# Where TensorE's combination and gather stand in an expert step, and which engine makes two low parts

## The reference, cut to what matters

```python
for e in range(N_EXPERTS):                      # 32 experts, D = 1024, FF = 512
    gate, up = jnp.split(z @ w_gate_up[e], 2, axis=-1)
    y = y + combine[..., e:e + 1] * ((jax.nn.silu(gate) * up) @ w_down[e])
return rms_norm(x + y, final_norm_g)
```

## Time and profile before

| | |
|---|---|
| median of 3 runs | 925.91 us |
| the profiled execution's own time | 929.3 us |
| its span | 927.5 us |
| TensorE matmul busy | 873.3 us (94%) |
| VectorE busy | 814.4 us (88%) |
| ScalarE busy | 621.7 us (67%) |
| 96 loads of expert weights, 2 MB each, median from issue to landing | 9.8 us |

### The profile page before, as it was taken

One profiled execution on the slowest core, in us unless ns is written; L12 is line 12 of the kernel. 1 busy time (PEld: TensorE's weight loads), 2 busy tenths in 40 slices (PEclk: granted clock), 3 DMA queues, 4 the chain that ended last, 5 costly groups with the idle time before them and its releaser, 6 DMA issues.

```text
span 927.5 us, 14508 instructions
## 1 busy us (share of the span) xinstructions
PE 873.3 (94%) x5734; PEld 751.2 (81%) x5734; DVE 814.4 (88%) x818; ACT 621.7 (67%) x537; POOL 11.0 (1%) x19
## 2 busy tenths in 40 slices
PE   5999999999999899868999999999999999999975
PEld 5999999999899899657877777777777877777764
DVE  5358999999867957488999999999999999999993
ACT  5563434345453573558888878888888878887882
POOL 0110000000000000020000000000000000000000
PEclk9999999999999999979999999999999999999997
DMA  9952545455443486518999999999999999999911
GB/s 379 374 183 97 210 155 194 170 184 194 159 155 119 182 317 267 211 37 327 384 400 399 411 395 407 398 411 400 401 408 408 396 400 406 409 398 396 423 66 45
DMA packets 20146, 270.64 MB, mean 292 GB/s; under 512 B 2192, under 2 KB 2448, under 8 KB 3856
## 3 DMA queue, kind: packets, MB, share of 16 engines
q1 hardware_dynamic: 19696, 268.59, 73.0%
q10 hardware_dynamic: 416, 1.57, 0.5%
HBM read 269.10 MB, written 1.05 MB: 291 GB/s over the span
## 4 chain that ended last, share of the span: by engine, by line
PE 48%; DVE 30%; issue 14%; ACT 6%; DMA 1%; DVEq 1%; SPq 0%; ACTq 0%
DVE lo L932 10%; PE ps L1317 10%; PE ps L1146 9%; PE ps L1147 9%; PE ps L1148 9%; DVE lo_last L932 7%; ACT hi L578 5%; PE ps L1305 3%; DVE lo L704 2%; DVE conv L791 2%; PE ps L1161 2%; PE ps L1163 2%; PE ps L1162 2%; DVE y_lo L1055 1%; DVE hT L1041 1%
## 5 line engine op out<-in xcount | busy, mean ns | idle before, releaser
L932 DVE TENSOR_TENSOR lo<-raw,hi 128x2048 fp32r<-128x2048 f32 x142 | 323.5, 2287 | 7.6 <-ACT hi L578 6.6
L578 ACT ACTIVATE hi<-raw 128x2048 fp32r<-128x2048 f32 x141 | 264.2, 1909 | 3.5 <-PE ps L1317 3.5
L1317 PE MATMUL ps<-hi,xeT 128*128 128x512 f32 x384 | 158.4, 412 | 15.1 <-DVE lo L932 11.2
L704 DVE TENSOR_TENSOR lo<-raw,hi 128x2048 fp32r<-128x2048 f32 x62 | 141.7, 2288 | 30.0 <-ACT hi L396 28.5
L1146 PE MATMUL ps<-inA,hi 128*128 128x256 f32 x576 | 165.1, 287 | 1.6 <-DVE lo L704 1.1
L1147 PE MATMUL ps<-inA,hi 128*128 128x256 f32 x576 | 163.8, 284 | 0.0
L1148 PE MATMUL ps<-inA,lo 128*128 128x256 f32 x576 | 163.7, 284 | 0.0
L396 ACT ACTIVATE hi<-raw 128x2048 fp32r<-128x2048 f32 x63 | 120.6, 1914 | 63.6 <-PE ps L1148 41.0
L1317 PE MATMUL ps<-lo,xeT 128*128 128x512 f32 x384 | 150.7, 392 | 0.0
L1146 PEld LDWEIGHTS ps<-inA,hi 128*128 128x128 f32 x576 | 111.4, 193 | 2.7 <-DVE lo L704 2.6
L1147 PEld LDWEIGHTS ps<-inA,hi 128*128 128x128 f32 x576 | 111.5, 194 | 0.1
(11 more groups left out here) (214 smaller groups left out, 1229.5 us busy)
## 6 DMA issues: line engine op xcount, KB each, us to landing
raw<-in_w_experts SPq DMA_DIRECT2D x96, 2048.0 KB, 9.8
raw<-in_w_dense SPq DMA_DIRECT2D x29, 2048.0 KB, 7.8
raw<-in_w_dense SPq DMA_DIRECT2D x2, 1024.0 KB, 8.1
x_sb<-in_x SPq DMA_DIRECT2D x1, 1024.0 KB, 4.8
mem_sb<-in_mem SPq DMA_DIRECT2D x1, 1024.0 KB, 15.5
x_again<-in_x ACTq DMA_DIRECT2D x1, 1024.0 KB, 5.0
out<-x SPq DMA_DIRECT2D x2, 512.0 KB, 2.7
ffn_row<-in_rows ACTq DMA_DIRECT2D x1, 512.0 KB, 7.4
```

The lines of the kernel that those rows point to most:

```text
L578: nc.scalar.activation(expert_half(hi, N0), raw_flat(slot, k % 2), ACT.Copy).then_inc(hi_made, 1)
L704: nc.vector.tensor_tensor(conv_half(lo, N), raw_half(slot, h), conv_half(hi, N).bitcast(f32), ALU.subtract).then_inc(lo_made, 1)
L932: nc.vector.tensor_tensor(expert_half(lo, N0), raw_flat(expert_slot(m), k % 2), expert_half(hi, N0).bitcast(f32), ALU.subtract).then_inc(l ...
L1317: last = mm(dst, xeT[:, par, 4 * (k % 2) + kt, k // 2 % 2, :], expert_half(w, N)[:, kt * 512:(kt + 1) * 512], start=(k % 4 == 0 and kt == ...
```

## The change

Two low parts leave VectorE. For the rows, TensorE multiplies the high part with minus the identity and adds this onto the gathered sum, which is still in its bank (`xeT_remainder`, between halves 6 and 7, two matmuls of 512 columns); the bank then holds the low part, and ScalarE copies it out (`expert_xeT_lo`). The same is done for the output (`y_remainder`, between halves 2 and 3, two matmuls; `y_out_lo` on ScalarE, two copies). ScalarE makes the minus identity once, before step 0. The combination is cut in two, after half 3 and after half 4; the gather is cut in 3 + 5 of its 8 tiles, before and after half 5. `hT_hi` and `hT_lo` move from the end of a step to behind high (low) 4 of the next, and `y_hi` behind high 2. After the loop three of the four down halves come before step 14's combination. For this the gather sets `start` only for the first tile of each bank, since the later minus identity matmuls add to all of it.

TensorE after: halves 0, 1, 2, output's remainder, 3, combination (first half), 4, combination (second half), gather 0 to 2, 5, gather 3 to 7, weights and `put`, 6, rows' remainder, 7, and on as before. ScalarE after: high 2, `y_hi`, 3, 4, `hT_hi`, 5, 6, two `y_lo`, gate out, 7, 8, rows' high part, `put`, 9, rows' low part, 10, up out, 11, SiLU, 12, 13. VectorE after: low 2, 3, 4, `hT_lo`, 5 to 8, slot weights, 9, `pick`, 10, 11, 12, `h`, 13.

The diff, cut to its core:

```diff
@@ -603,16 +606,28 @@
             nc.scalar.activation(ident_bf[:, :], ident, ACT.Copy).then_inc(ident_made, 1)
+            nc.scalar.activation(minus_ident[:, :], ident, ACT.Copy, scale=-1.0).then_inc(ident_made, 1)
             expert_xeT(0, 0)
-            def y_out(i, used):
+            def expert_xeT_lo(i, par):
+                act.wait_ge(xeT_rest, i)
+                nc.scalar.activation(xeT[:, par, :, :, SLOTS:2 * SLOTS], gathered_view(), ACT.Copy).then_inc(xeT_made, 1)
+            def y_out_lo(count):
+                act.wait_ge(y_rest, count)
+                for g in range(2):
+                    nc.scalar.activation(y_lo[g][:, :], DN[g], ACT.Copy).then_inc(y_lo_made, 1)
+            def y_out(used):
...
-            def hT_hi(i):
-                act.wait_ge(h_made, i + 1)
+            def hT_hi(count):
+                act.wait_ge(h_made, count)
                 nc.scalar.activation(hT[:, :, :, 0:SLOTS], h_sb[:, :, :, :], ACT.Copy).then_inc(h_hi, 1)
@@ -628,24 +643,35 @@
                 if start:
-                    more(4, 5)
+                    more(4, 5, 6)
                 else:
-                    more(2, 3, 4, 5)
+                    more(2)
+                    if not isinstance(j, int):
+                        y_out(used)
+                    more(3, 4)
+                    act.wait_ge(half_used, used)
+                    hT_hi(i)
+                    more(5, 6)
+                    if not isinstance(j, int):
+                        y_out_lo(i - 1)
                 act.wait_ge(half_used, used + 4)
...
                 nc.scalar.activation(gu_sb[:, 0:FF], G0, ACT.Copy).then_inc(gate_out, 1)
-                more(6, 7)
                 if start:
+                    more(7)
                     act.wait_ge(comb_made, 1)
                     act.wait_ge(loops_made, 1)
+                else:
+                    more(7, 8)
                 expert_xeT(i + 1, (r + 1) % 2)
-                more(8)
...
                 nc.scalar.activation(put[:, r, :], G0[:, T:2 * T], ACT.Copy).then_inc(put_made, 1)
+                if start:
+                    more(8)
                 more(9)
+                expert_xeT_lo(i + 1, (r + 1) % 2)
                 if not start:
@@ -660,10 +686,6 @@
                     more(12, 13)
-                    act.wait_ge(half_used, used + 12)
-                hT_hi(i)
-                if not start:
-                    y_out(i - 1, used + 12)
@@ -672,7 +694,11 @@
                 step(j, 1)
+            act.wait_ge(half_used, 2 * STEP * last_turn + (DENSE + 2 * STEP - 4))
+            hT_hi(2 * last_turn + 2)
+            y_out(2 * STEP * last_turn + (DENSE + 2 * STEP - 4))
             expert_hi(last_turn, 2 * STEP - 4, 2)
+            y_out_lo(2 * last_turn + 1)
             expert_hi(last_turn, 2 * STEP - 4, 3)
@@ -1034,10 +1060,10 @@
-            def hT_lo(i):
-                dve.wait_ge(h_made, i + 1)
-                dve.wait_ge(h_hi, i + 1)
+            def hT_lo(count):
+                dve.wait_ge(h_made, count)
+                dve.wait_ge(h_hi, count)
                 nc.vector.tensor_tensor(hT[:, :, :, SLOTS:2 * SLOTS], h_sb[:, :, :, :], hT[:, :, :, 0:SLOTS].bitcast(f32),
@@ -1068,10 +1094,14 @@
                 else:
-                    more(2, 3, 4, 5, 6, 7)
-                xeT_lo(i + 1, (r + 1) % 2)
+                    more(2)
+                    more(3, 4)
+                    hT_lo(i)
+                    more(5, 6, 7, 8)
                 slot_weights(i, r)
-                more(8, 9)
+                if start:
+                    more(8)
+                more(9)
                 make_pick(r, slice(r + 2, r + 3) if first else bass.ds(2 * j + (r + 2), 1))
@@ -1083,11 +1113,6 @@
                     more(13)
-                hT_lo(i)
-                if not start:
-                    dve.wait_ge(y_hi_made, i)
-                    for g in range(2):
-                        y_out_lo(g, DN[g], y_lo_made)
@@ -1096,6 +1121,7 @@
                 step(j, 1)
+            hT_lo(2 * last_turn + 2)
             expert_lo(last_turn, 2 * STEP - 4, 2)
@@ -1293,10 +1319,10 @@
-            def gather(i, par):
+            def gather(i, par, tiles=range(KT)):
                 pe.wait_ge(pick_made, i + 1)
-                for c in range(KT):
+                for c in tiles:
                     dst = ps[:, 6 + c // 4, c % 4 * 2 * SLOTS:(c % 4 + 1) * 2 * SLOTS]
@@ -1304,8 +1330,9 @@
                                   pick2[:, par, t, 0:2 * SLOTS],
-                                  start=(k == 0), stop=(k == 3 * TT - 1))
-                last.then_inc(gathered, 1)
+                                  start=(k == 0 and c % 4 == 0), stop=(k == 3 * TT - 1), skip_group_check=True)
+                if c == KT - 1:
+                    last.then_inc(gathered, 1)
@@ -1333,14 +1360,31 @@
-            def combine(par):
-                for t in range(TT):
+            def combine(par, tiles=range(TT)):
+                for t in tiles:
                     for g in range(2):
...
+            def y_remainder(count):
+                pe.wait_ge(y_hi_made, count)
+                for g in range(2):
+                    last = mm(DN[g], minus_ident[:, :], y_hi[:, g * 512:(g + 1) * 512], start=False, stop=True,
+                              skip_group_check=True)
+                last.then_inc(y_rest, 1)
+            def xeT_remainder(i, par):
+                pe.wait_ge(xeT_hi, i + 1)
+                for a in range(2):
+                    last = mm(DN[a], minus_ident[:, :],
+                              xeT[:, par, 4 * a:4 * a + 4, :, 0:SLOTS].rearrange("p c x s -> p (c x) s"),
+                              start=False, stop=True, skip_group_check=True)
+                last.then_inc(xeT_rest, 1)
@@ -1356,19 +1400,24 @@
                 gate_or_up(j, at_half, 1, r)
+                gate_or_up(j, at_half, 2, r)
+                if not first:
+                    y_remainder(i - 1)
+                gate_or_up(j, at_half, 3, r)
                 if not first:
...
                     pe.wait_ge(y_lo_made, 2 * i - 2)
-                    combine(r)
-                gate_or_up(j, at_half, 2, r)
-                gate_or_up(j, at_half, 3, r)
-                gather(i + 1, (r + 1) % 2)
+                    combine(r, (0,))
                 if not start:
...
                 gate_or_up(j, at_half, 4, r)
+                if not first:
+                    combine(r, (1,))
+                gather(i + 1, (r + 1) % 2, (0, 1, 2))
                 gate_or_up(j, at_half, 5, r)
+                gather(i + 1, (r + 1) % 2, (3, 4, 5, 6, 7))
@@ -1388,6 +1437,9 @@
                 gate_or_up(j, at_half, 6, r)
+                if start:
+                    pe.wait_ge(ident_made, 2)
+                xeT_remainder(i + 1, (r + 1) % 2)
                 gate_or_up(j, at_half, 7, r)
@@ -1418,14 +1470,17 @@
+            y_remainder(2 * last_turn + 1)
+            pe.wait_ge(silu_made, 2 * last_turn + 2)
+            pe.wait_ge(h_made, 2 * last_turn + 2)
+            pe.wait_ge(h_lo, 2 * last_turn + 2)
+            down(last_turn, 2 * STEP - 4, 0, 0, (G0, G1))
+            down(last_turn, 2 * STEP - 4, 1, 0, (G0, G1))
+            down(last_turn, 2 * STEP - 4, 2, 1, (G0, G1))
             pe.wait_ge(put_made, 2 * last_turn + 1)
...
             combine(0)
-            pe.wait_ge(silu_made, 2 * last_turn + 2)
-            pe.wait_ge(h_made, 2 * last_turn + 2)
-            pe.wait_ge(h_lo, 2 * last_turn + 2)
-            for k in range(4):
-                down(last_turn, 2 * STEP - 4, k, k // 2, (G0, G1))
+            down(last_turn, 2 * STEP - 4, 3, 1, (G0, G1))
             pe.wait_ge(put_made, 2 * last_turn + 2)
...
             combine(1)
```

More of the change, by code:

```diff
@@ L147, in hybrid_moe_kernel @@
         fold2 = at("fold2", S0 + 2 * KB + 512, [2, SLOTS])
+        minus_ident = at("minus_ident", S0 + 4 * KB, [P], r32)
         part = at("part", S0, [2, T])
@@ L210, in hybrid_moe_kernel @@
         silu_made, h_made, h_hi, h_lo = map(sem, ("silu_made", "h_made", "h_hi", "h_lo"))
+        xeT_rest, y_rest = sem("xeT_rest"), sem("y_rest")
         y_hi_made, y_lo_made, combined = map(sem, ("y_hi_made", "y_lo_made", "combined"))
```

## The result

The changed kernel takes **941.0 us** (median of 4 runs, 940.36 to 941.75) against 926.38 us for the kernel before, measured again beside it (4 runs, 925.41 to 927.47). The ratio is 1.0158, with a 95% interval of 1.014 to 1.0175: slower by 1.6%, inside the predicted range and 1.3 us above the predicted 939.7. Its profiled execution took 940.36 us with a span of 938.6 us.

A forecast was written before the change was run, and what follows sets the result against it. VectorE was taken to bound the kernel at 31.20 us a step. 929.3 + 17.9 (loop) + 0.5 (first steps) - 4.6 (end) = 943.1 us, or 939.7 against the median; range 932 to 947.

The forecast's parts named there:

- What bounded the kernel before: In the loop, VectorE sets the pace at 31.20 us a step and TensorE follows; about 2.3 comes off VectorE.
- The new wait and its cycle: In each loop step, TensorE waits about 2 us for y_lo; the cycle through ScalarE and the gather takes 32.48 us.
- The second cycle: TensorE's own cycle in the loop: half 11, y_hi, y_lo, rest of the step, 32.2 us; the longer one was taken.
- In the loop: Steps 2 to 15: each 1.28 us longer than 31.20, times 14, +17.9 us.
- Steps 0 and 1: Before the loop: later gather and rows plus two remainder matmuls cost +0.5 us, bounds -1 and +3.
- The end to the last combination: After the loop: halves now precede the combination, 14.6 us instead of 19.1, -4.6; -1.9 if the clock drops.
- the 3.4 by which I corrected its time to the median: Whole kernel: the profiled execution is 3.4 us above the runs' median 925.91, so 943.1 becomes 939.7.
- Nothing of VectorE's is late next: In the loop after the change, lows 9 to 12 come 2 us or more ahead of TensorE.
- The faster case: In the loop, y_lo copies are ready when half 3 ends, TensorE sets the pace: 912 us; chance 0.08.
- The falling clock: Clock falls in every loop step after the gap, 2.7 us a step, 38 more, 977 us; chance 0.04.

The follow-up runs named there:

- run 9: Kernel before with only the rows' low part moved (minus identity on TensorE between halves 6 and 7, copy on ScalarE behind high 9, gather's start flags): 913.88 us.
- run 1: Changed kernel with ScalarE's two y_lo copies moved from behind high 6 to ahead of high 5: 933.22 us.
- run 2: Changed kernel with ScalarE's two y_lo copies moved between high 5 and high 6: 923.84 us.
- run 3: Changed kernel with ScalarE's two y_lo copies moved later, behind the gate's copy and high 7: 1005.52 us.
- run 4: Changed kernel with TensorE running all of the combination after half 4, ScalarE untouched: 923.99 us.
- run 6: Changed kernel with ScalarE's high 9 moved ahead of the rows' high part, y_lo still behind high 6: 935.89 us.
- run 7: Changed kernel with both the y_lo copies between high 5 and high 6 and high 9 ahead of the rows' high part: 909.73 us.
- run 10: Run 7 with VectorE's product h moved behind low 13: 912.75 us.
- run 8: Changed kernel with the combination of step 14's output ahead of the last four down halves again, loop untouched: 943.38 us.

## Why the prediction was right

**What bounded the kernel before** was read rightly: run 9 takes 1.13 us a step off VectorE and nothing else, and the step falls by 0.83.

**The new wait and its cycle** were the step that decided, and they held. Predicted: y_lo 9.75 after y_hi starts, measured 9.73; ScalarE 23.74, measured 23.69; TensorE's way to the gather's end with both hand-overs 8.74, measured 8.65; idle before the rows about 3.5, measured 3.6; TensorE's wait 1.5 to 2.3, measured 1.44 to 1.52 in the 14 steps, at the low edge; VectorE's busy share about 0.90, measured 0.89 (89.29 of the 100 us shown). The period was 32.48 on paper and 32.33. Runs 1 to 4 and 6 move y_lo, its consumer or what stands ahead of it, and the wait goes (runs 1, 2, 4), grows (3) or stays (6) as the theory says, with the same instructions throughout. The second cycle, 32.2 on paper, fits the 32.03 of run 6, where a cycle by way of the rows' remainder is as long.

**The terms of the sum**, from one profiled execution to the other. In the loop, between the first half of step 2 (462.22 before, 460.72 after) and the end of step 15's half 11 (898.81, 913.88): 436.6 to 453.2, +16.6, predicted +17.9. Steps 0 and 1, from VectorE's first low part of the rows (410.20, 406.85): +1.85, predicted +0.5 with bounds of -1 and +3. Nearly all of it, 1.73, is in step 0: ScalarE's copy of the up sum now stands behind the later gather and the rows' low part, and TensorE waits 1.18 for it. The end to the last combination: -4.5, predicted -4.6. From there to the end +0.55, by the clock; not foreseen. Together +14.5, where I had +13.8, and the medians differ by 14.6. That the total is so close is in part luck: -1.3 in the loop and +1.35 in the first two steps cancel. A slip in the tail changed nothing: 2.85, 9.3 and 2.3 make 14.45, not 14.6. The two profiled executions differ by 11.1 only, because the one after is 3.35 ahead where the expert part begins, after code that the change doesn't touch. Over the profiled executions of this study that point lies anywhere from 406.4 to 410.2, and the one before had the latest: this fits the 3.4 by which I corrected its time to the median. The second latest, run 9's at 409.71, was also 2.3 above its own median.

**"Nothing of VectorE's is late next"** was right for the changed kernel and wrong for its neighbours: VectorE's slot weights behind low 8 make a cycle of 31.02, hidden under 32.33. I had not laid it out. It made my expectations of runs 2 and 4 too good by 6 and 7 us and is part of the 18 in run 1, where the y_lo copies also waited for the remainder. In the changed kernel VectorE already idles 2.45 us a step there, between the slot weights and low 9.

**Rivals.** The faster case (912) needed y_lo by the end of half 3. Run 2 meets just this condition and takes 923.84, since TensorE does not set the pace then; so the price was wrong for this condition alone, and about right (909.7) once run 7 also moved high 9. The falling clock did not occur at gaps of 1.5, and did at 3.78 in run 3, at some 2.0 us a step where I had 2.7. Its evidence was read too kindly in two places: the gap of 1.75 is in step 1, which is written out, and not in the loop, and the row with the clock of 1.00 around the gap of 2.17 ends 0.1 us after it (the matmuls behind it do start 0.23 apart). The Trainium skill, page TensorE: Matmul & The Clock Gate, section HAM oscillation, describes the same: repeated waits between bursts that throttle each burst anew. By that rule, the trace of run 3 agrees (0.50 to 0.69 after each gap), and the changed kernel's loop shows no fall at its shorter gaps.

## What to carry to other kernels

Work taken off the busiest engine is worth what the next longest cycle leaves of it, and in a program with written orders that cycle is found by walking from a wait through each engine's queue back to the same wait, not by adding up busy times. When a producer moves to another engine, look at what stands ahead of it in that engine's queue and how long its consumer can go on: here two small groups moved on ScalarE turned +1.6% into -1.8%. After each fix walk the cycles again; the next one was 1.3 us of a step away (32.33 to 31.02), then 0.4 (to 30.58).

## What the runs showed of the hardware beyond that

A wait of TensorE that recurs every 32 us left the clock at 1.00 in all 14 steps when it was 1.5 us (the changed kernel), and lowered it to 0.50 to 0.69 over some 5 us in all 14 when it was 3.78 (run 3).

Between these two lengths the gap alone does not tell. At the end of the kernel the same gap of 2.17 stands before the same eight matmuls in all 13 profiled executions: in eleven, that of run 9 with its old end among them, the clock fell within the eight, and in those of the kernel before and of run 10 it did not. So the +0.55 above is not shown to come from the change. In run 8 a gap of 2.04 was followed by 0.64; it came two matmuls after another gap of 1.71, which by itself, in the changed kernel, left the clock at 1.00. And in step 1 of the changed kernel the clock fell after two gaps of 1.18 and 0.85 with eight small matmuls between them; in the kernel before, where only the second gap is there, it stayed at 1.00. The rows of the changed kernel (two of TensorE's timeline, then one of the table of windows):

```profile
428.67 1.10 PE L1459 MATMUL ps<-cst,gu_sb 128*128 128x64 f32 x8 [1.18 <-ACT gu_sb L680]
430.63 0.47 PE L1344 MATMUL ps<-hi,xeT 128*128 128x512 f32 x1 [0.85 <-issue]
...
432.00:434.00 2.00, 2.00 (x7) 1.52 (x6) 1.64 (x1) 2.00 (x2) 0.00 (x0) 0.50 0.83 328
```

This fall cost little: from the second gap's end to step 2 are 30.09 us, against 29.97 before, where TensorE waits 1.75 for a low half instead. What decides at gaps of about 2 was not tried.
